# Four columns of room behind each half tile of the split activations h, in one layer of a hybrid trunk

## What is computed

```python
h = rmsnorm(x, g_mix_pre)
z = h @ w_in                                   # 1024 x 3080
...                                            # conv group A, mLSTM group B
x = x + rmsnorm(concat(A, B) @ w_out, g_mix_post)
up = rmsnorm(x, g_ffn_pre) @ w_up              # 1024 x 5632
up = causal_dwconv(up, ffn_buf, w_conv_ffn, b_conv_ffn)
f = gelu(up[..., :D_FF]) * up[..., D_FF:]
x = x + rmsnorm(f @ w_down, g_ffn_post)
x = x + (p @ w_ple) * sigmoid(rmsnorm(x, g_ple) @ w_ple_gate)
```

## Time and profile before

| | us |
|---|---|
| median of 3 runs | 2705.51 |
| lowest, highest | 2704.6, 2708.81 |
| span of the profiled execution | 2707.0 |
| TensorE matmuls busy | 2676.2 |
| VectorE busy | 1729.9 |
| ScalarE busy | 921.2 |
| GpSimd busy | 237.0 |

### The profile page before, as it was taken

How to read it: one execution, slowest core, us unless ns; L and a number is a source line. 1 busy time by engine, 2 the same in 40 slices (tenths; PEclk the granted TensorE clock), 3 DMA queues, 4 the chain that set the end, 5 groups by cost and what they waited for, 6 DMA issues and landing times.

```text
span 2707.0 us, 37694 instructions
## 1 busy us (share of the span) xinstructions
PE 2676.2 (99%) x14549; PEld 2589.0 (96%) x14549; DVE 1729.9 (64%) x3699; ACT 921.2 (34%) x1932; POOL 237.0 (9%) x180
## 2 busy tenths in 40 slices
PE   9999999999999999999999999999999999999999
PEld 7989999999999999999999999999999998899998
DVE  8975898865566665555665664756866636472645
ACT  5464434453432122443321233532112425211113
POOL 4432515230000000000000000000000000000000
PEclk9999999999999999999999999999999999999999
DMA  9857989877566666565666666566666676466665
GB/s 329 318 192 272 361 333 364 324 276 297 187 230 231 231 233 232 206 253 202 230 228 235 231 226 254 193 220 227 229 233 231 213 285 145 171 240 231 233 232 203
DMA packets 125117, 660.59 MB, mean 244 GB/s; under 512 B 22010, under 2 KB 22654, under 8 KB 55182
## 3 DMA queue, kind: packets, MB, share of 16 engines
q1 hardware_dynamic: 111150, 628.29, 64.3%
q10 hardware_dynamic: 13792, 29.92, 3.4%
HBM read 533.04 MB, written 125.11 MB: 243 GB/s over the span
## 4 chain that ended last, share of the span: by engine, by line
PE 92%; DVE 4%; ACT 2%; DMA 1%; issue 1%; POOL 0%; SPq 0%; DVEq 0%; ACTq 0%; POOLq 0%
PE proj L673 29%; PE proj L674 28%; PE proj L675 28%; PE m L673 1%; PE m L674 1%; PE m L675 1%; DMA w_split<-w_kept 1%; PE m L857 1%; PE m L890 1%; PE m L891 0%; PE m L851 0%; PE m L868 0%; DMA w_raw<-in_w_units 0%; PE m L719 0%; DVE cv L1848 0%
## 5 line engine op out<-in xcount | busy, mean ns | idle before, releaser
L673 PE MATMUL proj<-h_split,w_split 128*128 128x416 f32 x2704 | 969.7, 359 | 4.1 <-DVE h_split L1782 1.9
L674 PE MATMUL proj<-h_split,w_split 128*128 128x416 f32 x2704 | 947.2, 350 | 0.0
L675 PE MATMUL proj<-h_split,w_split 128*128 128x416 f32 x2704 | 942.1, 348 | 0.0
L673 PE MATMUL proj<-f_split,w_split 128*128 128x416 f32 x1536 | 549.9, 358 | 10.3 <-POOL w_split L657 3.1
L674 PE MATMUL proj<-f_split,w_split 128*128 128x416 f32 x1536 | 539.2, 351 | 0.0
L675 PE MATMUL proj<-f_split,w_split 128*128 128x416 f32 x1536 | 536.1, 349 | 0.0
L673 PEld LDWEIGHTS proj<-h_split,w_split 128*128 128x128 f32 x2704 | 507.3, 188 | 15.3 <-issue 5.7
L675 PEld LDWEIGHTS proj<-h_split,w_split 128*128 128x128 f32 x2704 | 508.2, 188 | 9.9
L674 PEld LDWEIGHTS proj<-h_split,w_split 128*128 128x128 f32 x2704 | 508.6, 188 | 3.5 <-issue 1.4
L673 PEld LDWEIGHTS proj<-f_split,w_split 128*128 128x128 f32 x1536 | 288.9, 188 | 26.1 <-issue 6.1
L1825 DVE SCALAR_TENSOR_TENSOR cv<-a_ext,vecs,cv 128x416 f32<-128x416 f32 (+1 forms) x480 | 304.9, 684 | 0.0
(11 more groups left out here) (308 smaller groups left out, 2285.5 us busy)
## 6 DMA issues: line engine op xcount, KB each, us to landing
w_split<-w_kept SPq DMA_DIRECT2D x430, 1024.0 KB, 4.8
w_kept<-w_split SPq DMA_DIRECT2D x108, 1024.0 KB, 6.6
w_raw<-in_w_units SPq DMA_DIRECT2D x216, 256.0 KB, 4.8
x_resid<-in_x ACTq DMA_DIRECT2D x5, 1664.0 KB, 12.5
out_y<-x_resid ACTq DMA_DIRECT2D x8, 832.0 KB, 7.7
rows<-in_x ACTq DMA_DIRECT2D x4, 832.0 KB, 7.0
w_raw<-in_x ACTq DMA_DIRECT2D x3, 832.0 KB, 8.7
qkv<-in_p ACTq DMA_DIRECT2D x5, 416.0 KB, 5.3
```

The lines of the kernel that those rows point to most:

```text
L673: mm(dst, w_hi, a_hi, start=first, stop=False)
L674: mm(dst, w_hi, a_lo, start=False, stop=False)
L675: return mm(dst, w_lo, a_hi, start=False, stop=last)
```

## The change

The tensor `h_split` gets T + 4 = 420 columns for each half tile, and the name `h` becomes a view of the first 416 of them. A half tile now takes 1680 bytes in a partition, which is 26 times 64 and 16 more. The half tiles of h so begin at 0, 16, 32 and 48 beyond a multiple of 64 in turn: the high half of tile k at 0 (k even) or 32 (k odd), its low half at 16 or 48. `h_split` grows by 16 x 16 = 256 bytes in a partition, and every tensor behind it moves up by 256 bytes, four times 64, so that their places modulo 64 stay. `f_split` lies ahead of it and does not move. Every instruction is the one that it was, on all five engines, in the same order and with the same waits; only addresses differ.

```diff
@@ -283,7 +283,7 @@
         with nc.sbuf_tensor("f_split", [P, FH, 2, T], F32R) as f:
             pass
         f_room = sb("f_room", [P, FH * 2 * T])
-        h = sb("h_split", [P, KD, 2, T], F32R)
+        h = sb("h_split", [P, KD, 2, T + 4], F32R)[:, :, :, 0:T]
         w = sb("w_split", [P, RING, 2, KD * P], F32R)
         wg = sb("wg_split", [P, 2, KD, GATES], F32R)
         with nc.sbuf_tensor("w_spare", [P, 2, KD * P], F32R) as w_spare:
```

## The result

The changed kernel takes **2712.28 us** (median of 14 runs, 2709.94 to 2715.03), the kernel before 2707.80 us in runs beside it (14 runs, 2703.18 to 2712.42). The ratio is **1.0018, with an interval of 1.0011 to 1.0025**: slower by 4.5 us, small but not nothing. The prediction's 2705.5 was the median of three of these 14 runs of the kernel before; so of the 6.8 us between it and 2712.28, 2.3 us are the base and 4.5 us the change. The profiled execution has a span of 2709.8 us, against 2707.0.

A forecast was written before the change was run, and what follows sets the result against it. TensorE's split matmuls, their number times the start-to-start distance, were taken to bound the kernel. Terms summed to 0 (-3.1 to 4.9 us beside the matmuls), giving 2705.5 us, range 2697 to 2722 at 0.80; no change had 0.73.

The forecast's parts named there:

- the matmuls that read h: 8328 split matmuls on h, some 5552 newly starting off 64 bytes; claimed cost zero.
- The bounds: Limits for the h matmuls: 40 us slower if ragged starts cost 7.3 ns, 110 us gained if the 13.2 ns vanished.
- The first row: Float32 matmuls of L868 and L891, at various places off 64 bytes, take 273 and 272 ns: no visible cost.
- The second row: Gate matmuls, weights at 0, 16, 32, 48 with h at 0, no faster or slower: relative place doesn't matter.
- Not the weight load: TensorE's 188.9 ns distance isn't set by loading weights: gates load 36 columns in 112 ns, yet matmuls take 353 against 354.
- This loss is all that a change of addresses could give back: On TensorE, float32r's 188.9 ns against bf16's 175.7 loses 13.2 ns per matmul, the most that places could return.
- The check inside the profile: Unmoved f_split as control: forecast still 503 matmuls in 95 us on h, 742 in 140 us on f.
- The writers: ScalarE copies and VectorE subtractions writing 112 half tiles of either kind: zero, at worst 1.8 us, off the path.
- the ring's 256 bytes: Weight buffer w_split moved by 256 bytes: zero, or 3.1 us either way if TensorE's waiting for loads vanished or doubled.
- The ragged start: Rival: 5552 h matmuls pay up to 7.3 ns for starting off the grid, 40 us, 2745; chance 0.15.
- The clash of equal places: Rival: neighbouring half tiles at equal residues cause the 13.2 ns loss; all gone 2596, a third 2669; chance 0.12.
- only 16 bytes count: Rival: places matter only on a 16-byte grid, so nothing changed for h; 2705.5, the forecast itself.

The follow-up runs named there:

- M0 W0: Series of identical float32r matmuls behind the kernel before, moving operand (M) and weights (W) both pushed by 0 bytes: 188.3 ns at 416 columns.
- the series of 256, 384 and 512 columns: Series of one float32r matmul repeated at each width, appended to the kernel before: 120.0, 173.3 and 226.7 ns.
- the run on the ring alone: Kernel before with an unused 64-column tensor behind h_split, moving w_split and what follows by 256 bytes, h unchanged: 2707.39 us, ratio 0.9999.
- the runs with 32 and 224 bytes: Kernel before with the weight ring and all behind it moved by 32 bytes: 2730.85 us, ratio 1.0079; by 224 bytes: 2686.56 us, ratio 0.9915.
- in the kernel's order: Kernel before plus 28 series of 84 matmuls walking seven tiles (high, low, high half), both operands pushed by fixed bytes: 188.9 ns with no push.
- the tiles of the series: Seven tiles walked as the kernel does, in series appended to the kernel before: 190.5 ns at pitch 1680; 188.9 at 1664, 1696, 1712 and 1728.
- the series at one place: Kernel before with 38 series of 60 to 126 float32r matmuls at its end, mostly repeating one fixed place: 188.3 ns unpushed, 186.7 moving operand at 16.

## Why the prediction was wrong

**The step that failed** is the one on the matmuls that read h, "Between these ends I take zero, for two rows". The bounds held the answer, -110 and +40 us around the measured 4.7, and the range held the time; the value in between was wrong, and with it the most likely case. In place of zero the runs showed 0.57 ns on each of 8328 matmuls, from h's new places, since the ring's move alone cost nothing; half of it comes with the tiles' pitch alone.

*The first row, fp32 matmuls off 64 bytes cost nothing*. I had said myself that fp32 is easier, and rested on it all the same. Those matmuls also compare places by median durations, the fault of the next point.

*The second row, "how weights and activations lie to each other doesn't matter"*. This is the very thing that matters, in the runs that moved the ring alone: 186.7 ns and 189.6 ns where before it was 188.9. The row I read gives a matmul's **duration**, 353 against 354 ns; the path is set by the **distance** between starts, and the two don't go together: after the change the median duration in the stretch fell from 354 to 352 while the distance rose by 0.57. For the gates' matmuls I had no distance at all; the trace of before gives 189.3 ns on average for 112 of them, which would not have settled it.

*"Not the weight load"* rested on the same row, but comes out right for the whole distance: with the same loads, 384 columns run at 173.3 ns. Whether the load has a part in the last 2 ns is not shown; 36 columns of weights in place of 128 bring a matmul at M0 W0 from 188.3 to 186.7 ns, but 64 columns don't.

*"This loss is all that a change of addresses could give back"*, 13.2 ns. The size is right at this width, and the series of 256, 384 and 512 columns show it as 13.3 ns in every matmul; but most of it stays at the best places too: 186.7 - 175.7 = 11.0 ns. With 128 columns of weights nothing came below 186.7 ns, so places could give back 2.2 ns here, not 13.2.

*The check inside the profile.* The stretch "of 140 us on f" was not wholly on f. By tile, the window of the earlier trace rows before has both (f_split, then h_split):

```profile
905.00:1045.00 140.00, 40.38 (x214) 1.00 0.65 230
```

```profile
905.00:1045.00 140.00, 99.89 (x528) 1.00 0.65 230
```

The conclusion stood, since the true stretches on f have 188.89 ns as well, but that row didn't show it. And counts of 503 in a window could hardly have shown a change of 0.3%; the forecast's own test, "if the distance on h changes by over 1 ns", was too coarse as well, since a change of 0.57 ns was enough.

**What was right.** TensorE's distance is the time, and no wait grew. The writers, DMA and the ring's 256 bytes are worth nothing (the run on the ring alone, 0.9999). f stayed.

**The rivals.** The ragged start came nearest in size, "13.2 / 26 = 0.5 ns for one more piece", but that is luck, for it is refuted as a mechanism: with all of h 32 bytes off the grid the kernel is 13.4 us faster. And L674, which it says is "worse hit than L673", is not the line whose duration grew most, as far as durations tell: its mean went from 350 ns to 351, that of L675, which reads a high half, from 348 to 353. L675 in the page of before:

```profile
L675 PE MATMUL proj<-h_split,w_split 128*128 128x416 f32 x2704 | 942.1, 348 | 0.0
```

The clash of equal places had the right idea, that places act on each other, but named the wrong partners, one half tile and the next instead of activations and weights, and the wrong modulus, 64 instead of 256. The sign fits no better: the change made neighbours differ and the kernel became slower; with all half tiles at equal places modulo 64, but 32 bytes on, it became faster. That only 16 bytes count, so that the change does nothing, is refuted by 1.0018, and more plainly by the runs with 32 and 224 bytes, all multiples of 16.

The Trainium skill ("SBUF — State Buffer", Who interferes with whom) says that TensorE reads its moving operand and its weights through two independent ports and never waits on anyone. The runs here disagree in so far as moving the weights' ring alone, by 224 or 32 bytes, made the same program 22 us faster or 22 us slower (more than half of the slower one is unexplained).

**What stays open.** That the distance between moving operand and weights modulo 256 decides, in the kernel's order and with weights on steps of 32 bytes, is shown from both sides; with weights off these steps, or at one place many times, it is not the whole rule. What collides physically, perhaps the load of the next weights beside the running stream, is a guess: moving the weights changes the distance, but 36, 64, 96 and 128 columns of them show no trend. Why a walk through the distances costs 0.28 ns and not the mean's 0.46, and why the change as a whole costs 0.57, is open. The order of the distances, or how low halves lie to high ones, seems to matter: at the pitch of 1712 bytes the tiles of the series walk through the same steps of 32 in another order (0, 96, 192, 32, 128, 224, 64), with low halves off steps of 32 as in the change, and take 188.9 ns, where the pitch of 1680 took 190.5 (the kernel's eight tiles: 189.4 to 189.5). No run varied either alone.

## What to carry to other kernels

Where TensorE runs float32r products back to back, it is worth trying other places of the weights against the activations: in this kernel a move by 32 or 224 bytes was worth some 0.8% either way, and a few columns of room ahead of one tensor set it. Here the best was one good distance for all tiles (32 bytes modulo 256). Measure it, since the rule behind it is known only in part. Read such effects from starts that lie hundreds of matmuls apart, since neither a matmul's duration nor a count of some 500 in a window shows half a nanosecond. And when a row is "easier" than the case in question, let it bound the term and not fix it.

## What the runs showed of the hardware

- Float32r matmuls of 256, 384 and 512 columns follow each other at 120.0, 173.3 and 226.7 ns, 13.3 ns beyond a constant sum for each column; 128 and 448 columns take more than that, 111.6 and 206.7 ns. The Trainium skill ("TensorE: Matmul & The Clock Gate", Back-to-back issue gap) gives N / 2.4 + 2.5 ns for the isolated gap of warm matmuls, 175.8 ns for 416 columns as an estimate, and says that it over-counts in a stream of loads and matmuls at large N; the bf16 matmuls' 175.7 agree with the formula, the float32r ones, at 186.7 at best, lie above it.
- A start of the moving operand 4 or 8 bytes beyond a multiple of 16 can be dear: 193.3 and 191.9 ns in the series at one place, against 186.7 at 16; in the kernel's order 194.5 and 192.5, but 188.9 at 12 bytes, as at 0.
- With both operands on steps of 16 bytes the distance at 416 columns is mostly one of a few levels (186.7, 187.8, 188.9, 190.0, 191.1 ns), with some between, and the same places can run at two of them in one execution: 189.6 and 193.3 ns with the ring 32 bytes on, 187.8 and 188.9 with the low halves 16 bytes off.
